# Last mixer's heads: where a pair of heads is gated on VectorE, and where ScalarE takes its leading part

## The reference, cut to what matters

```python
def _mlstm_readout(h, o, norm_w, w_out):
    bsz, nh, t_len, dv = h.shape
    h = h.transpose(0, 2, 1, 3)
    h = h * lax.rsqrt(jnp.mean(h * h, axis=-1, keepdims=True) + EPS)
    h = h.reshape(bsz, t_len, nh * dv).astype(o.dtype) * norm_w
    return (jax.nn.sigmoid(o) * h) @ w_out
```

## Time and profile before

| what | us |
|---|---|
| median of 3 runs | 1995.83 (1995.27 to 1997.36) |
| the profiled execution, its own time | 1995.16 |
| its span in the profile | 1993.3 |
| TensorE busy | 1954.5 (98%) |
| VectorE busy | 1390.3 (70%) |
| ScalarE busy | 885.7 (44%) |
| GpSimd busy | 254.6 (13%) |
| mean granted TensorE clock | 0.997 |

### The profile page before, as it was taken

The page is one execution under the profiler, slowest core; times in us unless marked ns, Lnnn a source line. Parts: engine busy times, 40 slices in busy tenths (PEclk is TensorE's granted clock), DMA queues, the critical chain, the costliest instruction groups (busy, mean ns, idle before and its releaser), DMA issues.

```text
span 1993.3 us, 27409 instructions
## 1 busy us (share of the span) xinstructions
PE 1954.5 (98%) x10285; PEld 1619.2 (81%) x10285; DVE 1390.3 (70%) x2220; ACT 885.7 (44%) x1513; POOL 254.6 (13%) x333
## 2 busy tenths in 40 slices
PE   7999999999999999999999999999999999989998
PEld 3877788788888777888889888878888878878887
DVE  5899767788766645488987665766755467566655
ACT  3433354333333453575554224524333353556554
POOL 2101011111111200411101001011110021321000
PEclk9999999999999999999999999999999999999999
DMA  8434225655653540378865432545555245227753
GB/s 307 133 100 134 85 96 180 201 181 178 195 177 96 172 159 22 108 232 282 262 206 161 135 109 74 198 147 171 167 171 157 68 154 180 81 98 232 223 184 110
DMA packets 191859, 315.19 MB, mean 158 GB/s; under 512 B 14653, under 2 KB 114328, under 8 KB 191728
## 3 DMA queue, kind: packets, MB, share of 16 engines
q1 hardware_dynamic: 162512, 210.09, 32.7%
q0 software_dynamic: 29216, 103.36, 17.0%
HBM read 312.35 MB, written 1.05 MB: 157 GB/s over the span
## 4 chain that ended last, share of the span: by engine, by line
PE 90%; DVE 4%; issue 2%; ACT 1%; POOL 1%; DMA 1%; SPq 0%; POOLq 0%; DVEq 0%; ACTq 0%
PE bank L683 26%; PE bank L690 24%; PE bank L689 24%; PE bank L693 9%; PE bank L688 2%; PE bank L686 2%; PE bank L738 1%; PE bank L762 1%; DVE acc L2203 1%; DVE wl L2178 1%; DMA raw<-in_ada_w 1%; PE bank L1068 0%; POOL wl L3111 0%; ACT junk L1579 0%; DVE X L2314 0%
## 5 line engine op out<-in xcount | busy, mean ns | idle before, releaser
L1563 ACT ACTIVATE wh<-raw 128x1024 fp32r<-128x1024 f32 (+4 forms) x390 | 399.4, 1031 | 593.7 <-PE bank L690 556.6
L2178 DVE TENSOR_TENSOR wl<-raw,wh 128x1024 fp32r<-128x1024 f32 (+3 forms) x372 | 440.0, 1189 | 266.5 <-ACT wh L1563 265.1
L683 PE MATMUL bank<-HH,wh 128*128 128x256 f32 (+1 forms) x1552 | 516.5, 333 | 2.9 <-DVE HH L2297 2.0
L690 PE MATMUL bank<-HH,wl 128*128 128x512 f32 (+1 forms) x1232 | 415.1, 337 | 0.0
L689 PE MATMUL bank<-HL,wh 128*128 128x512 f32 (+1 forms) x1232 | 414.9, 337 | 0.0
L2203 DVE SCALAR_TENSOR_TENSOR acc<-ada,sc,acc 128x512 f32<-128x512 f32 x518 | 362.2, 745 | 2.3
L683 PEld LDWEIGHTS bank<-HH,wh 128*128 128x128 f32 x1552 | 294.5, 190 | 32.0 <-issue 6.0
L683 PE MATMUL bank<-wh,UH 128*128 128x512 f32 x768 | 306.5, 399 | 0.0
L689 PE MATMUL bank<-wl,UH 128*128 128x512 f32 x768 | 303.3, 395 | 0.0
L690 PE MATMUL bank<-wh,UL 128*128 128x512 f32 x768 | 303.2, 395 | 0.0
L689 PEld LDWEIGHTS bank<-HL,wh 128*128 128x128 f32 x1232 | 232.5, 189 | 27.7 <-issue 2.2
(11 more groups left out here) (348 smaller groups left out, 2596.4 us busy)
## 6 DMA issues: line engine op xcount, KB each, us to landing
raw<-in_mlp_w SPq DMA_DIRECT2D x256, 512.0 KB, 4.4
ada<-in_mod_w POOLq DMA_DIRECT2D x96, 512.0 KB, 4.7
ada<-in_ada_w POOLq DMA_DIRECT2D x80, 512.0 KB, 4.6
raw<-in_ml_w_qkvo SPq DMA_DIRECT2D x28, 512.0 KB, 3.9
raw<-in_conv_w_in SPq DMA_DIRECT2D x24, 512.0 KB, 4.5
raw<-in_ada_w SPq DMA_DIRECT2D x12, 512.0 KB, 6.2
raw<-in_mla_w_o SPq DMA_DIRECT2D x8, 512.0 KB, 4.0
raw<-in_gla_w_v SPq DMA_DIRECT2D x8, 512.0 KB, 3.9
```

The lines of the kernel that those rows point to most:

```text
L683: pe.matmul(o, sh, mh, start=start, stop=False, skip_group_check=True)
L690: return pe.matmul(o, sl, mh, start=False, stop=stop, skip_group_check=True)
L1563: act.activation(k.wh[n % NSPL][:, 0:m], k.raw[(NDIRECT + n) % NRAW][:, 0:m], ACT.Copy).then_inc(*k.w_hi.up("w hi", n))
L2178: dve.tensor_tensor(k.wl[n % NSPL][:, 0:m], k.raw[(NDIRECT + n) % NRAW][:, 0:m], k.wh[n % NSPL][:, 0:m].bitcast(F32), ALU.subtract).then_i ...
```

## The change

Three moves, in turns 8, 9 and 10 and again in 12, 13 and 14, for the pairs 0 and 1 (the two last pairs are handled after the loop, as before):

- VectorE's `gated` goes from the end of turn 8 (12) to behind `front` of turn 9 (13), ahead of `weigh`;
- VectorE's `gated_low` goes from the end of turn 9 (13) to the end of turn 10 (14), behind `means` and `normed` of the next pair;
- ScalarE's `gated_high` goes from turn 8 (12), where `walk.take` stood behind it, to the end of turn 9 (13).

```diff
@@ ScalarE, the loop over steps @@
             if h and r:
                 over_den(h - 1)
                 head_squares(h - 1)
-            if j in (8, 12):
-                gated_high((j - 8) // 4)
+            if j in (9, 13):
+                gated_high((j - 9) // 4)
             if j < 2 or j % 2 == 0:
                 walk.take()
@@ VectorE, the loop over steps @@
             front(h, r)
             if j < 2 or j % 2 == 0:
                 walk.take()
+            if j in (9, 13):
+
+                gated((j - 9) // 4)
             weigh(h, r)
...
             if j in (6, 10, 14):
                 means((j - 6) // 4)
                 normed((j - 6) // 4)
-            if j in (8, 12):
-                gated((j - 8) // 4)
-            if j in (9, 13):
-                gated_low((j - 9) // 4)
+            if j in (10, 14):
+                gated_low((j - 10) // 4)
```

## The result

The changed kernel takes 1999.25 us, the median of 20 runs (1997.26 to 2004.11), against 1996.12 us for the kernel before, measured in 20 runs beside it (1993.33 to 1998.34). The ratio is 1.0017, 95% interval 1.0011 to 1.0023: 3.1 us or 0.17% slower (the interval is 2.2 to 4.6 us). The forecast was 2.5 us.

A forecast was written before the change was run, and what follows sets the result against it. TensorE has 90% of the chain, so only its waits in the last mixer's 16 turns could be gained. Terms: -1.5 + 2.7 - 1.86 + 2.7 = +2.04, clock +0.5, total +2.5: 1998.3 us, range 1994.5 to 2001.0.

The forecast's parts named there:

- `front` ahead of `gated`, +0.60 for `back`: Turn 9: gated runs behind front on VectorE, so TensorE's back of turn 8 comes 0.60 us later.
- m_T 1.46 earlier: Turn 8: with gated_high out of the way and o_out earlier, m_T waits only for its bank, 1.46 us earlier.
- Turn 10's exponential and `normed`, -1.5: Turn 10: the exponential, and with it normed of the next pair, comes 1.5 us earlier.
- HL behind `normed`, +2.7: Turns 10 and 14: gated_low is blocked by GpSimd's wl, delaying the next turn's front by 2.7 us each time.
- HL keeps its place: Rival: VectorE issues gated_low ahead of wl in turns 10 and 14, 0.60 us each; 1993.7 us in all, chance 0.13.
- blocked once: Rival: wl blocks gated_low in only one of the two places; sum 0, 1995.8 us, chance 0.08.
- `back` of turn 12 1.8 late: Turn 12: TensorE's back comes 1.8 us late, following the late front of turn 11.
- The last m_S, a wait of 2.9: Turn 15: TensorE waits 2.9 us before back for the last weigh, which follows the late front.
- The second pair's -0.36 for the missing half clock: Turns 12 to 14: a half-clock stretch in the profile before goes away, making the second pair's gain -1.86 us.
- +2.04: Sum of the forecast's terms over both pairs before the clock term: -1.5 + 2.7 - 1.86 + 2.7, in us.
- The clock, +0.5: TensorE's longer idle stretches before mD and back of turn 12 and back of turn 15 may bring half clock: +0.5 us.
- the rival of half clock in turns 12 to 14: Rival: idle ahead of back of turn 12 halves TensorE's clock for following matmuls; 4.0 us slower, 2000.5 with first stretch, chance 0.18.

The follow-up runs named there:

- the last experiment: Kernel with gated_low between front and weigh of turns 10, 14, gate and wl waiting for normed; added: wl behind the loop after gate(3), root(3), normed(3). 1992.09 us.

## Why the prediction was right

**`front` ahead of `gated`, +0.60 for `back`: right.** `back` of turn 8 came 0.59 later (1737.54 less the offset 3.58, against 1733.37).

**m_T 1.46 earlier: right,** 1.45 (1738.29 less 3.58, against 1736.16). **Turn 10's exponential and `normed`, -1.5: right,** 1.51 (1745.29 less 3.58, against 1743.22).

**HL behind `normed`, +2.7: right in mechanism and size,** 2.75 and 2.82, and it is this term that makes a gain into a loss. The runs with GpSimd held back and with HL elsewhere show that it is wl's presence that costs. The rivals "HL keeps its place" and "blocked once" fall: both rows of HL are long.

**`back` of turn 12 1.8 late: right,** 1.82 (1757.26 less 3.58, against 1751.86). **The last m_S, a wait of 2.9: the number is right, 3.00, in part by luck.** TensorE was ready 1.09 us early and not 0.65 (1768.30 less 3.58, against 1765.81), and m_S came 1.70 late and not 2.04 (1771.30 less 3.58, against 1766.02); both errors are those of the next term, and in this wait they cancel.

**The second pair's -0.36 for the missing half clock: mis-sized.** Turn 14's exponential came 0.63 early against a forecast of 0.65, but `normed` of pair 2 then gained 0.45 more, because in the profile before `back` of turn 13 on VectorE had also waited for the slow TensorE. The profile so shows +1.7 over the turns (51.75 against 50.03 in the table), not +2.04. The step that fell short is the path from turn 14's exponential to `normed`, which the forecast took to be as long as before. This term belongs to the profile before, not to the change: a stretch of half clock that one execution had.

**The clock, +0.5: not shown term by term.** None of the three idle stretches that the forecast priced brought half clock in the profile after; it has none in the turns. Taken without any on either side, before is 18.51 + 18.38 + 12.24 (the second is the first less the 0.13 that its `head_sum` was held by wl), 49.13, and the change 51.75: +2.6, where the forecast's own terms without half clock give -1.5 + 2.7 - 1.5 + 2.7 = 2.4. The two terms that rest on the clock, -0.36 and +0.5, nearly cancel in the forecast, so its total says little about either. Medians differ by 3.1, with 2.2 to 4.6 as interval. The runs' mean clocks point to more half clock in the change: 0.9957 over its 20 runs, against 0.9966 and 0.9968 in the 30 and 27 runs of before that stand beside the experiments. Within the 20 runs 0.001 less clock goes with 1.0 us more time (a fitted line). But the runs of before beside the change have no clocks on record, so whether this is the rest, and whether the longer idle stretches bring it about, stays open. That the rival of half clock in turns 12 to 14 can happen is seen in the run with GpSimd held back: there TensorE's `back` of turn 12, behind an idle stretch of 2.23 us, ran at 0.50:

```profile
1752.07 1.21 PE L693 MATMUL bank<-m_C,m_qT 128*128 128x129 f32 x4 [2.23 <-DVE tp L2993]
```

```profile
1752.00:1753.00 1.00, 0.93 (x4) 0.56 0.00 0
1753.00:1754.00 1.00, 1.00 (x7) 0.50 0.03 10
```

Its distance 1 to 2 was 19.08, where 16.95 + 0.60 would be the one without: 1.5, close to the 1.6 that the forecast priced. As the main cause it wasn't needed.

## What to carry to other kernels

When an instruction moves, ask which operation of another engine it will stand beside at its new place, and whether both read SBUF, not only which queue it stands in: one of 0.7 us, which costs 0.6 by its length, cost 2.8 us twice, because it came just behind the start of a 2.4 us operation of GpSimd. The row to look for is one that is longer than its kind and ends just behind an operation of the other engine. The rest of the change was sound: with HL in VectorE's idle time of turn 10 the same moves give 3.9 us (2.0 to 5.4; 3.0 by the table) in place of a loss of 3.1, so measure the parts before the whole is dropped.

## What the runs showed of the hardware that was not expected

- GpSimd's waiting operation comes in between two VectorE operations that stand ready one behind the other. It was read from one sequence before; it held in all four HL rows that had wl beside them (2.83 and 2.86 in the change, 2.83 and 2.87 in the run with HL's move alone) as in the tail's `head_sum`. The Trainium skill's page "SBUF — State Buffer", section "Who interferes with whom", says that the second to come is blocked wholly. The trace agrees: wl's row is 2.77 us long, and HL's ends 0.55 behind it. VectorE, which had just run `normed`, didn't get on to HL ahead of the waiting wl. The row of the engine that is held counts as busy, so the wait doesn't show as idle time.
- Half-clock stretches come and go between executions in places whose instructions are the same (180 to 200 and 860 to 880 us above), most of them worth 0.9 to 1.7 us where TensorE is in the chain. A difference of 3 us between two spans can be made of these alone, and comparing runs at equal granted clock, as at the last experiment, or distances inside a stage takes them out.
